# Eight blocks on one core: the first mixer's columns reordered, attention placed between the parts of its input projection, output projection split by branch

## What is computed

```python
def hybrid_mixer(u, w_in, forget_bias, ..., w_out, cos, sin):
    proj = u @ w_in                         # 256 x 1024 @ 1024 x 3792
    (aq, ak, av, iq, ik, iw, bq, bk, bv, cq, ck, cv, cf, cg) = jnp.split(proj, splits, axis=-1)
    aq, ak = rope(rms_norm(aq)), rope(rms_norm(ak))          # 4 heads of 64, one shared key head
    iq, ik = rope(iq), rope(ik)                              # 8 index heads, one key head
    o_a = dsa_attention(aq, ak, av, iq, ik, iw)              # keys: the 64 with the highest index score
    o_b = causal_attention(rope(rms_norm(bq)), rope(rms_norm(bk)), bv)       # 4 heads
    log_f = log_sigmoid(cf + forget_bias)
    o_c = forgetting_attention(rms_norm(cq), rms_norm(ck), cv, log_f)        # 8 heads
    o_c = o_c * sigmoid(cg)
    return concatenate([o_a, o_b, o_c], -1) @ w_out          # 256 x 1024 @ 1024 x 1024
```

## Time and profile before

| | us |
|---|---|
| median of 3 runs | 2043.59 (2043.04 to 2054.57) |
| profiled execution, its own time | 2051.39 |
| its span, first to last instruction | 2049.6 |
| TensorE busy | 1935.5 (94%) |
| VectorE busy | 1394.5 (68%) |
| ScalarE busy | 944.3 (46%) |
| GpSimd busy | 151.4 (7%) |
| mean granted clock of TensorE | 0.969 |

### The profile page before, as it was taken

The page is one execution under the profiler, slowest core; times in us unless marked ns, Lnnn a source line. Parts: engine busy times, 40 slices in busy tenths (PEclk is TensorE's granted clock), DMA queues, the critical chain, the costliest instruction groups (busy, mean ns, idle before and its releaser), DMA issues.

```text
span 2049.6 us, 26068 instructions
## 1 busy us (share of the span) xinstructions
PE 1935.5 (94%) x10928; PEld 1673.8 (82%) x10928; DVE 1394.5 (68%) x1548; ACT 944.3 (46%) x1154; POOL 151.4 (7%) x124
## 2 busy tenths in 40 slices
PE   7999988999999999799999999989997999989997
PEld 6888866988888888679888878878886878878886
DVE  6876678677678776767876446658765446668764
ACT  5444453444444444525444564544443464544442
POOL 0000640000000007200000001100000001100000
PEclk9999998999999999879999999989998999999998
DMA  7555450355555555304545543324554443424552
GB/s 272 185 175 195 164 181 1 124 191 180 184 191 194 180 177 188 134 1 161 189 176 194 185 166 135 128 103 175 188 188 159 144 171 121 157 103 164 191 184 77
DMA packets 47204, 326.77 MB, mean 159 GB/s; under 512 B 5488, under 2 KB 5488, under 8 KB 10864
## 3 DMA queue, kind: packets, MB, share of 16 engines
q1 hardware_dynamic: 46368, 322.78, 44.0%
q10 hardware_dynamic: 720, 2.33, 0.3%
HBM read 324.04 MB, written 1.05 MB: 159 GB/s over the span
## 4 chain that ended last, share of the span: by engine, by line
PE 76%; issue 9%; DVE 7%; POOL 5%; ACT 3%; DMA 0%; POOLq 0%; SPq 0%; ACTq 0%; DVEq 0%
PE ps L452 31%; PE ps L453 16%; PE ps L446 6%; PE ps L448 6%; PE ps L447 6%; ACT w_hi L265 1%; PE ps L644 1%; DVE w_lo L272 1%; POOL arena L1626 1%; PE ps L591 1%; PE ps L593 1%; PE ps L592 1%; POOL arena L1627 1%; POOL arena L1625 1%; PE ps L613 1%
## 5 line engine op out<-in xcount | busy, mean ns | idle before, releaser
L272 DVE TENSOR_TENSOR w_lo<-raw,w_hi 128x2048 fp32r<-128x2048 f32 (+3 forms) x314 | 705.7, 2251 | 334.1 <-ACT w_hi L265 331.7
L265 ACT CAST w_hi<-raw 128x2048 fp32r<-128x2048 f32 (+3 forms) x314 | 583.7, 1861 | 687.6 <-PE ps L453 431.1
L452 PE MATMUL ps<-x_hl,w_hi 128*128 128x512 f32 x2112 | 746.0, 398 | 33.3 <-DVE x_hl L1157 18.1
L453 PE MATMUL ps<-x_hl,w_lo 128*128 128x256 f32 x2112 | 594.8, 282 | 0.0
L452 PEld LDWEIGHTS ps<-x_hl,w_hi 128*128 128x128 f32 x2112 | 399.5, 189 | 125.7 <-issue 33.9
L453 PEld LDWEIGHTS ps<-x_hl,w_lo 128*128 128x128 f32 x2112 | 402.8, 191 | 0.0
L452 PE MATMUL ps<-hid_hl,w_hi 128*128 128x512 f32 x1056 | 371.0, 394 | 0.0
L446 PE MATMUL ps<-w_hi,x_hl 128*128 128x512 f32 (+3 forms) x744 | 287.7, 387 | 15.2 <-DVE x_hl L1157 8.4
L453 PE MATMUL ps<-hid_hl,w_lo 128*128 128x256 f32 x1056 | 299.1, 283 | 0.0
L447 PE MATMUL ps<-w_lo,x_hl 128*128 128x512 f32 (+3 forms) x744 | 283.6, 381 | 0.0
L448 PE MATMUL ps<-w_hi,x_hl 128*128 128x512 f32 (+3 forms) x744 | 283.5, 381 | 0.0
...
## 6 DMA issues: line engine op xcount, KB each, us to landing
...
```

What stands on the lines that cost most here:

```text
L265: nc.scalar.copy(w_hi[:, i % RING, 0:n_of(i)], raw[:, i % RING, 0:n_of(i)]).then_inc(high_ready, 1)
L272: nc.vector.tensor_tensor(w_lo[:, s, 0:n], raw[:, s, 0:n], w_hi[:, s, 0:n].bitcast(F32), ALU.subtract).then_inc(low_ready, 1)
L452: nc.tensor.matmul(ps[:, bank, :], w_h, hl.rearrange("p x n -> p (x n)"), start=start, stop=False, skip_group_check=True)
L453: return nc.tensor.matmul(ps[:, bank, 0:SEQ], w_l, hl[:, 0, :], start=False, stop=stop, skip_group_check=True)
```

## The change

**Columns and parts.** `w_in`'s columns are put in another order on the host: C_Q, I_Q, then A_Q, A_K, A_V, I_K, I_W, C_F (464 together), C_K, C_V, B_Q with B_K, B_V with half of C_G, and the other 256 of C_G. So there are 15 parts as before, fourteen half parts of which two are 464 wide, and one of 256 columns with all eight chunks. The output projection's c half stays two parts of 512 columns; its other half is cut by k: one part of 1024 columns for a's two chunks, one for b's.

**TensorE.** `attend` is kept for the second mixer only. In the first, `after_part(m)` issues pieces behind part m: index units behind parts 8 and 9; then in each step `turn_p(i)`, `scores(i + 1)`, `weigh(i)`; batches 5 to 7 between the parts of the output projection. The order of batches is c, c, a, b. All scores use banks 0 and 1, all weights one buffer (`p1`, `pT1`).

**ScalarE.** In each step: `evacuate` of a finished group, the pieces' work, then `split_hi(i0 + m + 3)`; before, the split stood first. It takes over the squares of the heads (`group_squares`), the nine rows from the cumulative sums, and the second transposed block of a batch (`turned_p`); the gains of c's q and k become the scale of `qk_copy`. The sigmoid of the gate runs in place behind part 14.

**VectorE.** In each step the pieces' work, then `split_lo`, then top-8 rounds. **GpSimd.** The rotations in the new order, and the sum of the next norm's squares.

```diff
-A_Q, A_K, A_V, I_Q, I_K, I_W = 0, 256, 320, 384, 896, 960
-B_Q, B_K, B_V = 968, 1224, 1480
-C_Q, C_K, C_V, C_F, C_G = 1736, 2248, 2760, 3272, 3280
+
+MIX1 = (("C_Q", 1736, 512), ("I_Q", 384, 512), ("A_Q", 0, 256), ("A_K", 256, 64), ("A_V", 320, 64), ("I_K", 896, 64),
+        ("I_W", 960, 8), ("C_F", 3272, 8), ("C_K", 2248, 512), ("C_V", 2760, 512), ("B_Q", 968, 256), ("B_K", 1224, 256),
+        ("B_V", 1480, 256), ("C_G", 3280, 512))
+MIX1_FROM = np.concatenate([np.arange(a, a + n) for _, a, n in MIX1])
+C_Q, I_Q, A_Q, A_K, A_V, I_K, I_W, C_F, C_K, C_V, B_Q, B_K, B_V, C_G = (
+    sum(n for _, _, n in MIX1[:i]) for i in range(len(MIX1)))
...
-WIN1 = column_parts(IN1)
-WOUT1 = [(c, 512, k, 4) for k in (4, 0) for c in (0, 512)]
+WIN1 = column_parts([512, 512, 464, 512, 512, 512, 512, 256])
+WOUT1 = [(0, 512, 4, 4), (512, 512, 4, 4), (0, 1024, 0, 2), (0, 1024, 2, 2)]
...
-        QK_UNITS = [((2 * u, 2 * u + 1), r) for u, r in enumerate(
-            [("rope_ready", 1), ("rope_ready", 2), ("rope_ready", 2), ("rope_ready", 2), ("rope_ready", 3),
-             ("rope_ready", 3), ("cqk_ready", 1), ("cqk_ready", 1), ("cqk_ready", 2), ("cqk_ready", 2)])]
-
-        QK_AFTER = {7: (0, 1, 2, 3), 10: (4, 5), 13: (6, 7), 14: (8, 9)}
+        QK_UNITS = [((12, 13), ("cqk_ready", 1), 0), ((14, 15), ("cqk_ready", 1), 1), ((3, 4), ("rope_ready", 1), 2),
+                    ((5, 6), ("rope_ready", 1), 3), ((7,), ("rope_ready", 1), 0), ((16, 17), ("cqk_ready", 2), 0),
+                    ((18, 19), ("cqk_ready", 2), 1), ((0, 1), ("rope_ready", 2), 3), ((2,), ("rope_ready", 2), 3),
+                    ((8, 9), ("rope_ready", 3), 3), ((10, 11), ("rope_ready", 3), 3)]
+
+        IDX_BANK, IDX_LAST = (2, 3, 0, 2, 3, 2, 3, 2), (None, None, None, 0, 1, 3, 4, 5)
...
-                for n in range(4):
+                last = m == 3 or parts is WO2 and m == 2
-                    if m == 3:
-                        pe.wait_ge(read[0], read[1] + n + 1)
+                    if last and c >= 4:
+                        pe.wait_ge(read[0], read[1] + c - 3)
...
-                        first = m == 0 and k == 0
+                        nc.tensor.matmul(mixer_out(c), hs[0], mk[:, 0, :], start=m == 0 and k == 0, stop=False, skip_group_check=True)
-                        mm = nc.tensor.matmul(mixer_out(c), hs[1], mk[:, 0, :], start=False, stop=m >= 2 and k == kc - 1, skip_group_check=True)
-                    if m >= 2 and n < 3:
+                        mm = nc.tensor.matmul(mixer_out(c), hs[1], mk[:, 0, :], start=False, stop=last and k == kc - 1, skip_group_check=True)
+                    if last and n < n_all // P - 1:
```

TensorE, new in `mixer1`:

```diff
+                def turn_p(i):
+
+                    pe.wait_ge(S["exp_ready"], 4 * i + 4)
+                    if i:
...
+                def weigh(i):
+
+                    b = B1[i]
+                    pe.wait_ge(S["pT_ready"], i + 1)
+                    if b["qt"]:
+                        pe.wait_ge(S["pT2_ready"], (i + 1) // 2)
...
+                def after_part(m):
+                    if m == 4:
+                        qk_turn(0)
+                        qk_turn(1)
+                    if m == 7:
+                        pe.wait_ge(S["qkT_ready"], 1)
+                        for u in (2, 3, 4):
+                            qk_turn(u)
+                    if m == 8:
+                        pe.wait_ge(S["qkT_ready"], 5)
+                        for u in range(4):
+                            index_scores(u)
+                        pe.wait_ge(S["logf_ready"], 1)
...
+                    if m == 9:
+                        pe.wait_ge(S["relu_ready"], 3)
+                        qk_turn(5)
+                        pe.wait_ge(S["aug_ready"], 9)
+                        qk_turn(6)
+                        for u in range(4, 8):
+                            index_scores(u)
+                        pe.wait_ge(S["qkT_ready"], 7)
+                        scores(0)
+                    if m == 10:
+                        pe.wait_ge(S["relu_ready"], 8)
+                        turn_p(0)
+                        qk_turn(7)
+                        scores(1)
+                        pe.wait_ge(S["proj_ready"], 5)
+                        weigh(0)
+                    if m == 11:
+                        pe.wait_ge(S["qkT_ready"], 8)
+                        turn_p(1)
+                        scores(2)
+                        weigh(1)
+                    if m == 12:
+                        turn_p(2)
+                        qk_turn(8)
+                        scores(3)
+                        weigh(2)
+                    if m == 13:
+                        pe.wait_ge(S["qkT_ready"], 9)
+                        turn_p(3)
+                        scores(4)
+                        weigh(3)
+                    if m == 14:
+                        turn_p(4)
+                        scores(5)
+                        weigh(4)
+                        qk_turn(9)
+                        pe.wait_ge(S["qkT_ready"], 10)
+                        qk_turn(10)
+                        pe.wait_ge(S["proj_ready"], 8)
+                        turn([(S["gated"], 1), (S["gated"], 2)], 4, mixed, o=4 * P, bank=4)
+
...
+                    after_part(m)
+                project_out(i0 + 15, WOUT1, 0, 0, held={0: (S["tlo_ready"], 2)})
+                pe.wait_ge(S["qkT_ready"], 11)
+                turn_p(5)
+                scores(6)
+                weigh(5)
                 project_out(i0 + 15, WOUT1, 1)
+                turn([(S["o_ready"], 6)] * 2, 2, mixed, bank=3)
+                turn_p(6)
+                scores(7)
+                weigh(6)
                 project_out(i0 + 15, WOUT1, 2, 2)
-                project_out(i0 + 15, WOUT1, 3, read=(h_ready, H_BEFORE[s]))
+                turn_p(7)
+                weigh(7)
+                turn([(S["o_ready"], 8)] * 2, 2, mixed, o=2 * P, bank=3)
+                project_out(i0 + 15, WOUT1, 3, 3, read=(h_ready, H_BEFORE[s]))
```

ScalarE, new in `mixer1`:

```diff
+                def after_part(m):
+                    if m == 1:
+                        group_squares(C_Q, 512)
...
+                    if m == 8:
+                        act.wait_ge(S["gmean"], 3)
+                        for u in range(4):
+                            relu(u)
+                        act.wait_ge(S["cum_done"], 1)
+                        cum = ps[:, 1, 0:SEQ]
+                        nc.scalar.activation(k_aug, cum, ACT.Identity, scale=cst("k_mul"), bias=cst("k_add")).then_inc(S["aug_ready"], 1)
+                        for hd in range(8):
+                            nc.scalar.activation(q_aug[hd], cum, ACT.Identity, scale=cst("q_mul")[:, hd:hd + 1],
+                                                 bias=cst("q_add")[:, hd:hd + 1]).then_inc(S["aug_ready"], 1)
+                    if m == 9:
+                        qk_copy(5)
+                        qk_copy(6)
+                        for u in range(4, 8):
+                            relu(u)
+                        weights(0)
+                    if m == 10:
+                        qk_copy(7)
+                        weights(1)
+                    if m == 11:
+                        act.wait_ge(S["idx_used"], 8)
+                        group_squares(B_Q, 512)
+                        turned_p(1)
+                        weights(2)
+                    if m == 12:
+                        qk_copy(8)
+                        weights(3)
+                    if m == 13:
+                        turned_p(3)
+                        weights(4)
+                    if m == 14:
+                        for t in range(TT):
+                            gate = proj[:, t, C_G:C_G + 512]
+                            act.wait_ge(S["proj_ready"], 8)
+                            nc.scalar.activation(gate, gate, ACT.Sigmoid).then_inc(S["gate_ready"], 1)
+                        weights(5)
+                        qk_copy(9)
+                        qk_copy(10)
+                        turned_hi(mdue, 4, ones_col, m_hl, o=4, bank=4)
+
+                for m in range(len(WIN1)):
+                    evacuate(i0, WIN1, m, proj, [(0, IN1, ACT.Copy)])
+                    if m in (1, 5, 11):
+                        act.wait_ge(S["proj_ready"], groups_of(WIN1)[m][0] + 1)
+                    if m == 7:
+                        act.wait_ge(S["proj_ready"], 4)
+                    after_part(m)
+                    split_hi(act, i0 + m + 3)
+                turned_p(5)
+                weights(6)
                 split_hi(act, i0 + 18)
+                turned_hi(mdue, 2, ones_col, m_hl, bank=3)
+                weights(7)
                 split_hi(act, i0 + 19)
...
+                turned_p(7)
+                turned_hi(mdue, 2, ones_col, m_hl, o=2, bank=3)
                 split_hi(act, i0 + 20)
+                for c in range(KC):
                     next_x(s + 1, c)
                     square(h[:, c, :], c)
                 split_hi(act, i0 + 21)
```

(69 more changed lines are left out.)

410 lines of the change are left out of this document (226 added, 184 removed).

## The result

The changed kernel takes 2063.23 us (median of 14 runs, 2055.93 to 2070.23), the kernel before, run beside it, 2050.22 (14 runs, 2041.33 to 2055.83): a ratio of 1.0064, 95% interval 1.0045 to 1.0083. It is 13.0 us slower.

A forecast was written before the change was run, and what follows sets the result against it. TensorE was taken to bound the kernel: per first-type mixer 150.1 of work, 23.6 idle and 7.7 clock gave 181.4 us against 181.8, so 0.8 less over two mixers and a median of 2042.8, range 2014 to 2062.

The forecast's parts named there:

- Floor, 150.1: TensorE's work in one first-type mixer at 2.4 GHz throughout: 150.7 us before, less 0.6 for the new parts.
- Idle, 23.6: Sum of TensorE's walked waits in one first-type mixer: 23.6 us, against 18.7 before.
- Index unit 6: Behind part 9, TensorE waits for relu 5, queued on ScalarE behind other work: 3.3 us idle.
- `weigh(1)`: Behind part 11, TensorE waits for VectorE's copy, which follows the split and four rounds: 1.7 us idle.
- `weigh(3)`: Behind part 13, TensorE waits for VectorE's copy after maxima, exponentials, splits and four wide rounds: 3.5 us idle.
- `qk_turn(10)`: Before the output projection, TensorE waits for qkT 10, behind weights(5) on ScalarE: 2.7 us idle.
- scores(5): Behind part 14, TensorE waits for VectorE's second mask: 2.9 us idle.
- The clock, 7.7: Low-clock stretches after waits cost 7.7 us a mixer, with ends 0 and 15.
- The sum: Whole kernel: two mixers together 0.8 us faster, giving 2042.8 us as a median.
- Parts 0 to 7 and the rotation: Input projection's first parts run without a wait; the earlier 3.2 us wait for GpSimd's rotation goes.
- The slower rival: GpSimd and VectorE hold each other up at additions, splits and rotation: 10.9 us a mixer, 2064.6 in all; chance 0.10.
- The first rival: In both mixers the gaps close and the clock holds: 160 us a mixer, 2000 in all; chance 0.17.

The follow-up runs named there:

- e7: Changed kernel with VectorE's rounds earlier, other reorderings, and ready attention pieces moved into TensorE's waits around the output projection: 2013.13 us, ratio 0.9814 to the kernel before.
- e2: Changed kernel plus 74 unused 512-column products a mixer on TensorE, ahead of its longer waits: 2048.72 us, ratio 0.9996 to the kernel before.
- e9: e2 without its five unused products before weigh(1): 2052.42 us, ratio 1.0008 to the kernel before.
- e1: Changed kernel with VectorE's top-8 rounds of steps 10 to 13 done before it waits for ScalarE's split or GpSimd's root: 2041.81 us, ratio 0.9967.
- e5: Changed kernel with the seven square additions at the mixer's end back on VectorE, none on GpSimd: 2062.60 us, ratio 1.0062 to the kernel before.

## Why the prediction was wrong

It failed in one term, the clock, with a smaller error in TensorE's work; the waits were walked nearly right in sum. By its own steps:

- **Floor, 150.1.** Measured 152.0 in the changed kernel, 153.2 in e7 where no low clock blurs it. A half part costs 5.44 us in a row of parts, but 5.55 between pieces: its first product starts at 287.01 and the next piece at 292.56.

```profile
287.01 0.48 PE L469 MATMUL ps<-w_hi,x_hl 128*128 128x512 f32 x1
...
292.56 1.03 PE L715 MATMUL ps<-const,arena 128*128 128x128 f32 x8
```

  Eight half parts are followed by a piece now, three before: 0.6, which takes away the 0.6 that I had counted as saved. Error: 1.9 a mixer; the rest of it I haven't located, and some belongs to the division, which counts all busy time at the low clock as doubled.
- **Idle, 23.6.** Measured 21.4. Index unit 6: 3.3 forecast, 2.9. `weigh(1)`: 1.7, 1.3. `weigh(3)`: 3.5, 3.8. `qk_turn(10)`: 2.7, 3.5; ScalarE loads a table twice there, for the sigmoid and for the exponentials again, which my chain left out (the rows stand below). Output projection 2.4, 2.2. Last rows 1.8, 2.0. Small waits of the output parts 1.6, 1.5. Next stage 2.3, 1.4. Not on my list: 1.5 for the aug rows and 1.9 at `weigh(2)`. On it and absent: scores(5), 2.9, and the additions in the last part, 1.4. That the sum comes so near is partly luck: 4.3 that isn't there stands against 3.4 that I hadn't listed. e2 shows scores(5), 2.5 us, and the 2.3 of the next stage once the clock is up: these steps held for the clock at which they were computed, and the trace ran at another.

```profile
337.18 1.28 ACT L1183 ACT_TABLE_LOAD   x1
339.64 1.28 ACT L1125 ACT_TABLE_LOAD   x1
```

- **The clock, 7.7: the step that failed.** It measured 14.3 (10.8, 13.3, 15.8, 17.2), almost twice, and at the upper end of the 0 to 15 that I had kept. I charged one low stretch of 3.4 to most waits, half a one to `weigh(1)`, none to `weigh(3)`. The first mixer has 6.8 behind index unit 6 and behind `weigh(3)`, 3.4 behind `weigh(1)`, two of 3.4 around the projection's start, one in the last part; in the second trace it has 6.8 to 10.2 behind each. The earlier trace rows had shown an idle of 1.4 followed by 6.7 us low, and I still took the shorter case for each wait. The kernel before could have warned me: by my own figures 11.4 of clock stood there beside 18.7 of idle, and I put 7.7 beside 23.6. At the rate of before it would have been 14.4. e9 confirms the row, e1 and e2 that the waits are the cause.
- **The sum.** 6.6 for the clock and 1.9 for the work, less 2.2 of idle, is 6.3 a mixer, 12.6 in all; with the 6.6 by which the three runs stood low, 19.2 of the 20.4 between 2042.8 and 2063.2. The rest is that I compared with 181.8 a mixer, where two traces of the kernel before give 181.1: 1.3 in all.
- **Parts 0 to 7 and the rotation:** right, no wait at part 7.
- **The range and the rivals.** The slower rival's 2064.6 is near the time, but its mechanism is not what made it: the additions took under 0.9 us each, and e5 finds no time at the close. Something of it is in the trace at one place, GpSimd's root for b, which ran beside the split of part 14. GpSimd, then VectorE, in the first mixer:

```profile
302.12 4.88 POOL L1879 TENSOR_TENSOR stat<-stat,const 128x16 f32<-128x16 f32 x1 [42.74 <-DVE stat L1537]
```

```profile
301.95 2.28 DVE L277 TENSOR_TENSOR w_lo<-raw,w_hi 128x2048 fp32r<-128x2048 f32 x1
307.04 1.29 DVE L1543 TENSOR_TENSOR arena<-arena,stat 128x512 f32<-128x512 f32 x2 [2.80 <-POOL stat L1879]
```

  VectorE waited 2.80 for it with the rounds queued behind, and so came the wait of 1.9 at `weigh(2)`. In the second mixer the same root began just ahead of the split and not behind its start:

```profile
862.47 2.90 POOL L1879 TENSOR_TENSOR stat<-stat,const 128x16 f32<-128x16 f32 x1 [42.10 <-DVE stat L1537]
```

```profile
862.50 2.33 DVE L277 TENSOR_TENSOR w_lo<-raw,w_hi 128x2048 fp32r<-128x2048 f32 x1
```

  It took 2.90, and the wait at `weigh(2)` was 0.9 (in the second trace it took 4.88 in both mixers). So the two engines holding each other up cost 2.0 on the root and some 1.0 of idle where it happened, a small part of the 6.5 a mixer; the prediction had priced splits and additions, not a root. The first rival, that the gaps close and the clock holds (2000), did not come true for the change as made; e7, with other orders and places, has its mixers, 161.4 where I had written 160. What stood in the way first of all was the order on VectorE, as the prediction said of it.

Moving the pieces among the parts didn't help at first, because VectorE did the rounds, whose masks are wanted 12 us later or more, ahead of copies that TensorE wanted at once, and stood idle before them. e1 differs from the changed kernel in that alone and is 20 us faster by the two ratios.
